# Retention's forward rotation, decayed keys and gate: from GpSimd to the end of VectorE's slot

## What is computed

```python
def retention_scan(q, k, v, log_gamma, s0):
    ...
    def step(state, inp):
        qc, kc, vc = inp
        scores = jnp.einsum('bqhd,bkhd->bhqk', qc, kc) * decay
        intra = jnp.einsum('bhqk,bkhe->bqhe', scores, vc)
        cross = jnp.einsum('bqhd,bhde->bqhe', qc, state) * q_decay[None, :, :, None]
        new = (state * chunk_decay[None, :, None, None]
               + jnp.einsum('bkhd,bkhe->bhde', kc * k_decay[None, :, :, None], vc))
        return new, intra + cross

def retention_branch(q, k, v, log_gamma, s0_f, s0_b):
    k = k * HEAD_DIM ** -0.5
    o_f, s_f = retention_scan(q, k, v, log_gamma[0], s0_f)
    o_b, s_b = retention_scan(q[:, ::-1], k[:, ::-1], v[:, ::-1], log_gamma[1], s0_b)
    o = o_f + o_b[:, ::-1]
    mu = jnp.mean(o, axis=-1, keepdims=True)
    var = jnp.mean(jnp.square(o - mu), axis=-1, keepdims=True)
    o = (o - mu) * lax.rsqrt(var + EPS)
    return o, jnp.stack([s_f, s_b], axis=1)
```

## Time and profile before

| | us |
|---|---|
| median of 3 runs | 3651.34 (3649.44 to 3654.25) |
| profiled execution, its own time | 3649.23 |
| its span | 3647.1 |
| TensorE busy | 3494.6 (96%) |
| VectorE busy | 2819.9 (77%) |
| ScalarE busy | 1266.4 (35%) |
| GpSimd busy | 520.7 (14%) |
| chain that ended last: PE, DVE | 78%, 15% |
| mean granted TensorE clock | 0.978 of full speed |

### The profile page before, as it was taken

How to read it: one execution, slowest core, us unless ns; L and a number is a source line. 1 busy time by engine, 2 the same in 40 slices (tenths; PEclk the granted TensorE clock), 3 DMA queues, 4 the chain that set the end, 5 groups by cost and what they waited for, 6 DMA issues and landing times.

```text
span 3647.1 us, 70999 instructions
## 1 busy us (share of the span) xinstructions
PE 3494.6 (96%) x27041; PEld 2527.6 (69%) x27041; DVE 2819.9 (77%) x5662; ACT 1266.4 (35%) x3545; POOL 520.7 (14%) x798
## 2 busy tenths in 40 slices
PE   6998999999999998999999999999999999979998
PEld 5887888778864465555578878887888545655554
DVE  4666577647988999999955766784589799989996
ACT  3421333334431122444453123333344212224443
POOL 0210000100001255100000010001000015620000
PEclk9999999999999998999999999999999999979999
DMA  7443121232233334333432131213313333343332
GB/s 258 138 159 102 61 82 53 95 96 76 74 112 119 119 115 161 119 105 105 143 123 86 64 103 62 77 49 124 92 61 102 108 118 119 126 159 105 105 108 88
DMA packets 247264, 389.39 MB, mean 107 GB/s; under 512 B 30576, under 2 KB 175184, under 8 KB 246800
## 3 DMA queue, kind: packets, MB, share of 16 engines
q1 hardware_dynamic: 179600, 233.19, 20.7%
q0 software_dynamic: 39968, 122.30, 8.9%
q10 hardware_dynamic: 27360, 29.36, 2.6%
HBM read 264.42 MB, written 122.25 MB: 106 GB/s over the span
## 4 chain that ended last, share of the span: by engine, by line
PE 78%; DVE 15%; issue 3%; SPq 2%; DMA 1%; ACT 1%; DVEq 0%; POOL 0%; ACTq 0%; POOLq 0%
PE ps L1249 32%; PE ps L1653 14%; PE ps L1297 9%; PE ps L1436 4%; PE ps L1418 4%; PE ps L1405 3%; PE ps L1606 2%; DVE e_t L2382 2%; PE ps L1568 2%; PE ps L1409 2%; DVE e_t L2368 1%; PE ps L1471 1%; PE ps L1631 1%; PE ps L1365 1%; DVE ret_qd L2676 1%
## 5 line engine op out<-in xcount | busy, mean ns | idle before, releaser
L1249 PE MATMUL ps<-w_sb,s_t 128*128 128x256 f32 x3456 | 841.2, 386 | 26.3 <-DVE row_t L2292 13.6
L1249 PEld LDWEIGHTS ps<-w_sb,s_t 128*128 128x128 f32 x3456 | 630.6, 192 | 126.5 <-DVE s_t L2314 25.9
L1249 PE MATMUL ps<-w_sb,hT 128*128 128x256 f32 x2592 | 635.8, 385 | 3.8 <-ACT hT L1802 2.3
L1653 PE MATMUL ps<-wo_sb,mT 128*128 128x512 f32 x1152 | 534.4, 603 | 2.6 <-ACT mT L2049 2.6
L1297 PE MATMUL ps<-w_sb,hT 128*128 128x512 f32 x1152 | 528.5, 601 | 0.5 <-issue 0.3
L1249 PEld LDWEIGHTS ps<-w_sb,hT 128*128 128x128 f32 x2592 | 474.3, 192 | 72.9 <-issue 10.9
L2292 DVE TENSOR_TENSOR row_t<-ps,p_t 128x256 f32<-128x256 f32 x324 | 136.9, 423 | 350.9 <-PE ps L1249 347.0
L1297 PEld LDWEIGHTS ps<-w_sb,hT 128*128 128x128 f32 x1152 | 207.9, 190 | 213.8 <-issue 209.2
L1653 PEld LDWEIGHTS ps<-wo_sb,mT 128*128 128x128 f32 x1152 | 206.0, 190 | 206.8 <-issue 196.6
L1053 POOL DMA_DIRECT2D projected<-row_t x216 | 117.8, 546 | 1500.7 <-DVE row_t L2372 904.0
L1825 ACT ACTIVATE p_t<-ps 128x256 f32<-128x256 f32 x324 | 124.4, 384 | 542.7 <-PE ps L1249 540.1
(11 more groups left out here) (265 smaller groups left out, 5852.1 us busy)
## 6 DMA issues: line engine op xcount, KB each, us to landing
projected<-row_t POOLq DMA_DIRECT2D x288, 256.0 KB, 2.4
w_sb<-in_w_in ACTq DMA_DIRECT2D x40, 512.0 KB, 5.3
hg_raw<-projected SPq DMA_DIRECT2D x72, 256.0 KB, 4.4
out_streams<-y_t POOLq DMA_DIRECT2D x36, 512.0 KB, 4.8
wa<-in_w_ada SPq DMA_DIRECT2D x10, 1536.0 KB, 8.1
hg_braw<-projected SPq DMA_DIRECT2D x108, 128.0 KB, 2.5
hg_raw<-projected SPq DMA_DIRECT2D x36, 384.0 KB, 3.3
mx_t<-mixed SPq DMA_DIRECT2D x36, 384.0 KB, 5.6
```

What stands on the lines that cost most here:

```text
L1249: mm = nc.tensor.matmul(ps[:, (u.run + k) % 2, 0:HB], x[:, c], w_blk[:, at[w], c * HB:(c + 1) * HB], start=opens and c == 0, stop=(c == KH ...
L1653: mm = nc.tensor.matmul(ps[:, 6 + g, :], mT[:, t % 2, k, :], wo_sb[:, k, g * GRP:(g + 1) * GRP], start=(k == 0), stop=(k == KC - 1))
```

## The change

`rope_ret` and the multiplication of `gate_ret` leave GpSimd's queue and stand in VectorE's, with the same operands and shapes and the same waits. GpSimd keeps `store_ret`. On VectorE the gate of tile j - 2 stands before `scaled_ret(j - 1)`, and the rotation of tile j + 3 with its decayed keys at the end of the slot, behind `bounds_end`.

```diff
@@ gpsimd
-            own = Steps(pool, pool_step, l * NT * 3)
...
-            def rope_ret(j):
...
-            def gate_ret(j):
+            def store_ret(j):
                 u, b = l * NT + j, j % 2
-                pool.wait_ge(ret.scaled, u + 1)
-                pool.wait_ge(ret.gate_in[b], 16 * (l * NP + j // 2 + 1))
-                nc.gpsimd.tensor_tensor(ret.out_t[:, b], ret.out_t[:, b], ret.raw[:, b, 3 * GW:4 * GW], ALU.mult
-                                        ).then_inc(ret.out_ready, 1)
                 pool.wait_ge(ret.out_ready, u + 1)
                 pool.dma_start(mixed[tok(j), 2 * GW:3 * GW], ret.out_t[:, b]).then_inc(ret.stored[b], 16)
...
-                if 0 <= m - FORE + 3 < NT:
-                    rope_ret(m - FORE + 3)
                 if 0 <= m - FORE - 2 < NT:
-                    gate_ret(m - FORE - 2)
+                    store_ret(m - FORE - 2)
@@ vector
+            def rope_ret(j):
+
+                u, b = l * NT + j, j % 2
+                x, src, tab = ret.x[:, b], ret.raw[:, b, 0:2 * GW], ret.rope_t[:, b]
+                dve.wait_ge(ret.raw_in[b], 32 * (l * NP + j // 2 + 1))
+                if j >= 2:
+                    dve.wait_ge(ret.turned, u - 1)
+                need(dve, ret.kf_ready, u)
+                own.mark(nc.vector.tensor_tensor(x.rearrange("p (h n) -> p h n", n=HD), src.rearrange("p (h n) -> p h n", n=HD),
+                                                 tab[:, 0:HD].unsqueeze(1).broadcast_to([P, 2 * HEADS, HD]), ALU.mult))
+                for s in range(2):
...
+                    own.mark(nc.vector.tensor_tensor(y, other, sin.broadcast_to([P, 2 * HEADS, 2, HD // 4]), ALU.mult))
+                own.wait()
+                nc.vector.tensor_tensor(x, x, ret.tmp[:, :], ALU.add).then_inc(ret.x_ready, 1)
+                dve.wait_ge(ret.x_ready, u + 1)
+                if j >= 2:
+                    dve.wait_ge(ret.kv_done, u - 1)
+                nc.vector.tensor_tensor(ret.kd[:, b].rearrange("p (h n) -> p h n", n=HD),
...
+            def gate_ret(j):
+                u, b = l * NT + j, j % 2
+                dve.wait_ge(ret.scaled, u + 1)
+                dve.wait_ge(ret.gate_in[b], 16 * (l * NP + j // 2 + 1))
+                nc.vector.tensor_tensor(ret.out_t[:, b], ret.out_t[:, b], ret.raw[:, b, 3 * GW:4 * GW], ALU.mult
+                                        ).then_inc(ret.out_ready, 1)
...
                 if 0 <= j < NT:
                     variance_ret(j)
+                if 0 <= j - 2 < NT:
+                    gate_ret(j - 2)
                 if 0 <= j - 1 < NT:
                     scaled_ret(j - 1)
                 if piece and piece[0] == 6:
                     bounds_end(*piece)
+                if 0 <= j + 3 < NT:
+                    rope_ret(j + 3)
```

More of the change, by code:

```diff
@@ L651, in build @@
     ret.stored, ret.gate_in = pair("ret_stored"), pair("ret_gate_in")
-    ret.x_ready, pool_step, ret.turned, ret.xT_ready, ret.qd_ready, ret.centred, ret.squared, ret.scaled = (
-        sem(f"ret_{x}") for x in ("x_ready", "pool_step", "turned", "xT_ready", "qd_ready", "centred", "squared", "scaled"))
+    ret.x_ready, ret.turned, ret.xT_ready, ret.qd_ready, ret.centred, ret.squared, ret.scaled = (
+        sem(f"ret_{x}") for x in ("x_ready", "turned", "xT_ready", "qd_ready", "centred", "squared", "scaled"))
     hg.summed, hg.decayed = sem("hg_summed"), sem("hg_decayed")
@@ L1131, in save_states @@
                     pool.dma_start(dst, state[:, 0, g * HD:(g + 1) * HD]).then_inc(a.s_saved, 16)
-            def rope_ret(j):
+            def store_ret(j):
                 u, b = l * NT + j, j % 2
[L1136 to L1152, removed]
-                nc.gpsimd.tensor_tensor(ret.kd[:, b].rearrange("p (h n) -> p h n", n=HD),
-                                        ret.x[:, b, GW:2 * GW].rearrange("p (h n) -> p h n", n=HD),
-                                        ret.dec[:, D_KEY:D_KEY + HEADS].unsqueeze(2).broadcast_to([P, HEADS, HD]), ALU.mult
-                                        ).then_inc(ret.kf_ready, 1)
-            def gate_ret(j):
-                u, b = l * NT + j, j % 2
-                pool.wait_ge(ret.scaled, u + 1)
-                pool.wait_ge(ret.gate_in[b], 16 * (l * NP + j // 2 + 1))
-                nc.gpsimd.tensor_tensor(ret.out_t[:, b], ret.out_t[:, b], ret.raw[:, b, 3 * GW:4 * GW], ALU.mult
-                                        ).then_inc(ret.out_ready, 1)
                 pool.wait_ge(ret.out_ready, u + 1)
```

6 lines of the change are left out of this document (added).

## The result

| | median of the runs (lowest to highest) | span and time of the profiled one |
|---|---|---|
| before | 3652.8 us (3649.4 to 3656.9, 4 runs) | 3647.1, 3649.2 |
| after | 3685.2 us (3678.8 to 3687.7, 4 runs) | 3676.7, 3678.8 |

After over before is 1.0088, 95% interval 1.0076 to 1.0100: slower by 32 us in the medians, 29.6 in the two profiled spans. The forecast, 3663.0, lies 10 above this median of before; its own sum was 11.7.

The account below looks back on a forecast made before the run. It took TensorE to bound the steady slots, with VectorE barely keeping up. Layer terms of 4.8 and 6.9 us, together 11.7, on the profiled 3649.23 gave 3660.9; the median lying 2.1 above made 3663.0, range 3651 to 3677.

Parts of the forecast that it names:

- Removed and added, steady slots: Forward slots on VectorE: 5.5 us of stalls a pair go, 2.79 a slot added; pair 22.25 against TensorE's 22.02.
- the slack of 1.2: Middle slots: us by which the rotated tile is ready before TensorE wants it, shrinking by 0.23 a pair.
- The first sign that it named for being wrong: Middle of the pass: TensorE waiting for L2706 would show the forecast wrong; it put the cost there at 0.
- VectorE becomes the pace: Rival, steady slots: 0.4 us a slot dearer makes a pair 23.05, 5.2 us a layer more, 3673.4; chance 0.14.
- TensorE as the bound in the middle: Steady forward slots: TensorE sets the pace at 22.02 us a pair without waits, so the change costs 0 there.
- Begin: Slots 15 to 18: VectorE gets 2.1 us late in layer 0, 4.1 in layer 1, carried to slot 31.
- Tail, "relief 2.9, memsets 0.5": From slot 31, each layer: stalls that go, less four gates, give 2.9 us back; two memsets cost 0.5.
- The last store, 4.8, and last gate, 0.35: End of pass: tile 15's store lands later, making the last scaling 4.8 us later; last gate adds 0.35: 5.2 a layer.
- Sum: Both layers: 4.8 us more in layer 0 and 6.9 in layer 1, together 11.7.
- The cheap store: Rival, end of pass: tile 15's store lands in 2.5 us, 2.9 a layer less, 3657.2; 0.23 together with less lateness.
- The port: Rival, tail: GpSimd and VectorE shut each other out, memsets count their full 1.0 us: 3664.0; chance inside the forecast's.

Follow-up runs that it names:

- rope_only: The changed kernel with the gate's multiplication back on GpSimd with its store, rotation and keys staying on VectorE: 3668.0 us, 1.0041 of the kernel before.
- kd_three: The changed kernel with a third buffer for the decayed keys, so they wait for the kv_done of three tiles back: 3676.8 us, 1.0061 of before.
- square_first: The changed kernel with ScalarE's square of tiles 14 and 15 ahead of its takes of HGRN2's first tiles: 3677.6 us, 1.0070 of before.
- gate_load_first: The changed kernel with the last gate's load issued ahead of the 4 MB load of wo_sb on SP: 3682.6 us, 1.0081 of before.
- wo_on_act: The changed kernel with the 4 MB load of wo_sb issued on ScalarE's queue at slot 36 instead of SP's: 3678.3 us, 1.0065 of before.

## Why the prediction was right or wrong

It forecast slower by 10 us, in the range 3651 to 3677, and 3685.2 came: the direction was right, the size wrong by a factor of nearly three, outside the range. By its steps:

- *Removed and added, steady slots:* right in the prices. The stalls went whole (0.170 in all rows); light slot 9.06 of 9.06, pair 22.28 of 22.25. TensorE keeps its 22.03 at first; over the last pairs before slot 31 it follows VectorE, +0.4 and +0.6 in the middle column. The step's own numbers said so: 6.5 pairs x 0.23 = 1.5 is more than the slack of 1.2, yet it put the cost at 0. The first sign that it named for being wrong, TensorE waiting for L2706, is there in two slots of layer 0 and three of layer 1, growing to 0.87:

```profile
1393.29 0.42 PEld L1475 LDWEIGHTS ps<-ident,ret_x 128*128 128x128 f32 x4 [0.87 <-DVE ret_x L2706]
```

  "VectorE becomes the pace" came true to that extent only. In rope_only it is the pace: 22.83 a pair, +3.3 a layer.
- *TensorE as the bound in the middle*, against the Trainium skill's rule in "Perfetto Trace Analysis" (Identifying the Most-Contended Engine) that weight loads' busy share tells more than matmul busy time: the missing waits decided rightly here. In kd_three VectorE's pair is 22.28, longer than before's, and every pair of TensorE up to slot 31 stays at 22.02, the middle column at 0.
- *Begin:* right in kind for VectorE, by luck in the number of layer 0. VectorE entered slot 31 3.1 us later than before in layer 0, or 2.2 beyond the 0.9 that this execution was late at slot 15, against 2.0; in layer 1, 6.2 against 4.1, of which 1.7 is TensorE's clock. The forecast had TensorE gain 1.2 in layer 0, for its first wait would shrink, and lose 0.8 in layer 1 by a wait of `scores_ret(0)`. The first wait did shrink by 1.1, but the second came in both layers, 1.72 each. The 1.2 that TensorE nevertheless gained in layer 0 is the 1.7 of a slow stretch of its clock that before had there and after had not.
- *Tail, "relief 2.9, memsets 0.5":* wrong, and one of the two steps that made the miss. From slot 31 to the centring of tile 15 there was no relief but +0.6 and +0.1. Two things are missing in that step: the rotation of tile 17, 2.46 us in slot 32 ahead of HGRN2's levels, and ScalarE's square. The centring's stall did go, but before it had hidden ScalarE's chain, which ended 0.3 us ahead of its use (square at 1429.84 + 0.42 in before's trace, reduced at 1430.58). I counted the stall as gain without asking what was late next. square_first shows the second; the first is read from the rows alone, for no run took it out of the slot.
- *The last store, 4.8, and last gate, 0.35:* the store's term was right, +5.2 and +4.9, by the mechanism given; the landing was 5.9 for 5.4. The last gate's term is the other step that made the miss, and the larger one. The forecast said that the 4 MB load moves with the gate of tile 14, by some 8 us (it was 12.7), and used it only for the store. That the load of gate 17 stands behind it in SP's queue, and that VectorE now waits for that gate, was left out: 4.7 and 4.1 us on top of the 0.35. gate_load_first and wo_on_act show it: each takes the column to `hg_w` down to +0.3 in layer 0.
- *Sum.* To the centring of tile 15 the forecast was low by 3.2 and 4.6, at the store by 0.5 in both together, at the last gate by 8.8: 17.1, and 11.7 + 17.1 = 28.8 against the 28.7 of the marks. The rest of the 32 is 0.9 elsewhere, and that the profiled run was the fastest of four.
- *Rivals.* The cheap store did not come: 2.7 us is what it lands in when the 4 MB are behind it (gate_load_first), but then their own followers are late. *The port*, from the Trainium skill's "SBUF — State Buffer" (SBUF: two separate sides): after has no GpSimd operation but memsets and stores beside these slots, and no row of the stalled instruction above 0.17; rope_only has one operation a tile, and each stretches one VectorE row. By single rows the trace agrees with the rule's price, a whole instruction: the sum that began just ahead of GpSimd's 0.73 us took 0.68 longer. The means alone, 552 for 418, would not show it. The forecast's 0.5 for the memsets was not measured by itself.

## What to carry to other kernels

When an operation moves to another engine, follow the semaphore it raises to every queue that waits for it, and then read what is queued behind each of those: here one gate, made a slot later, started a 4 MB load 12.7 us later, and what stood behind that load cost nearly as much (4.7 and 4.1 us) as the wait one had seen (5.2 and 4.9). A stall that goes is a gain only up to the next chain that ends there: price the slot again with all engines. And where a stage ends in a tail that one engine bounds, lateness hidden in the middle is a debt: put operations behind waits that have been met (the keys one slot on, the gate behind its scaling only where the end needs it), and the change, with these reorderings and the square's, turned from 0.9% slower to 0.2% faster.
